# A fused two-block network on one core: four steps moved in the order of the work, and the output gates computed on 516 columns instead of 528

## The chip, the cores and the metric

The kernel runs on one core of one Trainium2 chip. The metric is the device time of one execution in microseconds (us), lower is better. A time is told as the median of several runs; the trace is one more execution, taken by the hardware profiler.

## The reference, cut to what matters

The input is a sequence of 512 positions of width 1024. A first block (gated linear attention, a gated convolution, windowed attention with sinks, then a feed-forward network with a causal convolution) gives 512 positions. The second block puts 16 meta tokens in front of them (528 positions) and computes two mixers side by side:

```
h = concat(meta_tokens, h)                       # 528 positions
q, f, i, g, z, xbc, dt = split(rmsnorm(h) @ w_in)
# HGRN2: 8 heads of 128, chunks, a state carried on
o = hgrn2(q, f, i);   y1 = rmsnorm_per_head(o) * norm_w * silu(g)
# Mamba-2: 16 heads of 64 in 2 groups
y = mamba2(silu(conv4(xbc)), softplus(dt));  y = y + d_skip * x
y = y * silu(z);      y2 = rmsnorm_per_group(y) * norm_w
h = h + concat(y1, y2) @ w_out
h = h + ffn(rmsnorm(h))                          # causal convolution, 3 taps
out = rmsnorm(h[16:])                            # the 512 positions
```

The gates g and z act position by position. Behind them only the last 4 of the 16 meta positions are read by anything that reaches the output, by way of the causal convolution of the last feed-forward network; the projections q, f, i and x, B, C feed states and need all 528.

## The kernel before

All is kept transposed, channels on the 128 partitions and positions along the free axis. The work is a list of groups (GROUPS, from plan()). One group is one output tile of 128 channels: for each 128x128 block of weights three matmuls in fp32r, w_hi·x_hi, w_lo·x_hi and w_hi·x_lo, added up in PSUM. Over 512 columns a product is one matmul; over 528 or 516 columns (from position USED = 12 on) it is two halves of 264 or 258 columns, so a group with 8 blocks issues 48 matmuls. columns(g) says which positions a group covers. The second block's groups use two PSUM slots in turn (slot_of): a group can only start when the group two before it has been evacuated.

Weights come in slabs of 8 blocks (128x1024). SyncE loads a slab into w_raw; ScalarE (ACT) copies it to w_hi in fp32r (split_until, in the profile w_hi at L911); VectorE (DVE) subtracts and stores w_lo (low_until, L1269); TensorE (PE) waits for w_lo. ACT does this at a group's own step (split_weights) and once more behind it (slab_behind), one slab further than DVE asks for at that step.

The order of everything is one hand-made list, STEPS, built by schedule(): a step "group" for each group, and behind it the stages put there. Every engine walks through the same list and issues its own part of each step, in order; semaphores tie the engines together. So a stage that stands earlier in the list stands ahead on all the engines that have a part in it.

Stages that matter here:

- hf, hq, hi, hg (heads 0 to 7): the four projections of an HGRN2 head. DVE evacuates each; ACT takes a tanh of hf, hq and hg. hf_fin, prep_ln, prep_sum and prep_exp make the decays; prep (behind hg) makes the keys and queries; head_a to head_d and head_v are the attention of the head before, on PE with copies on ACT and masks on DVE. head_b on PE waits for ACT's copies of head_a.
- second_start: part 4 is five memsets of VectorE (the largest 128x2560) that give zeros to tiles which prep and head_a of the second block fill; parts 0 to 3 scale h_res, two tiles each.
- SSM_ORDER and SSM_PIECES: the groups mz (gate), mx, mb, mc of Mamba-2, the output projections oh (of y1, 8 groups) and om (of y2, two halves of 4 blocks each), and the pieces behind each. "a t" (ssm_a): PE spreads the decays of tile t, ACT takes their exponentials, DVE multiplies; "b t" and "c t": states and outputs; "taps"/"silu": convolution; behind "c t" stand ssm_gate (DVE: two operations, the first waits for ACT's tanh of mz t), and ssm_sq (ACT squares, GpSimd adds up). ssm_sum(g) is the norm of a group: PE sums, ACT takes Ln and Exp (the root; exp_ln loads the table for it first). ssm_a(5) on PE waits for the root of group 0, since PSUM banks are shared.
- om: DVE waits for the root, multiplies the product with it (L1272), adds to h_res (L1269), and frees the slot.

Of the kernel before, what the change touches and what calls it, by code (L numbers as in the profile page):

```python
# [18 lines left out]
P = 128  # L19
D = 1024  # L20
KD = D // P
SEQ = 512
# [186 lines left out]
def schedule():  # L209
# [124 lines left out]
def program(nc, weights, xT, metaT, params, consts, cmask, w_alpha, outT):  # L334
    with ExitStack() as ctx:
# [253 lines left out]
        def _(pool):  # L589
            def ssm_sq(t):  # L590
# [5 lines left out]
                total = m_sq[:, t // 4, :]  # L596
                nc.gpsimd.tensor_tensor(total, total, m_z[t % 2], ALU.add).then_inc(ssm_sem["added"], 1)
# [7 lines left out]
        def _(pe):  # L605
# [145 lines left out]
            def head_d(n):  # L751
# [3 lines left out]
                if not gla:  # L755
                    last = mm(ps[:, 7, 416:432], ones[:, :], h_osq[:, 0:META])
# [125 lines left out]
            def ssm_sum(g):  # L882
# [4 lines left out]
                mm(ps[:, 6, 384:400], ones[:, :], m_sq[:, g, 0:META]).then_inc(S["sum"], 1)  # L887
# [15 lines left out]
        def _(act):  # L903
# [38 lines left out]
            def group(g):  # L942
                split_weights(g)
                kind, i, _ = GROUPS[g]
                if kind in ("gr", "hg"):
# [5 lines left out]
                    gate = (g_gate if kind == "gr" else h_gate)[:, i % 2, :]  # L951
                    evacuated(act, g)
                    f(c_a if kind == "gr" else h_thg, gate, ACT.Tanh, scale=0.5).then_inc(act_part, 1)
# [39 lines left out]
                elif kind == "mz":  # L993

                    if i >= 2:
                        act.wait_ge(ssm_sem["gated"], i - 1)
                    evacuated(act, g)
                    f(full[:, i % 2, :], m_z[i % 2], ACT.Tanh, scale=0.5).then_inc(act_part, 1)
# [10 lines left out]
            def group_and_slab(g):  # L1009
                group(g)  # L1010
                if GROUPS[g][0] != "hf":
# [138 lines left out]
            def head_d(n):  # L1150
# [4 lines left out]
                else:  # L1155
                    f(h_or[:, META:T2], ps[:, 6, :], ACT.Ln, scale=1.0 / P, bias=pc("eps"))
                    link(f(h_or[:, 0:META], ps[:, 7, 416:432], ACT.Ln, scale=1.0 / P, bias=pc("eps")))
                    last = f(h_or, h_or, ACT.Exp, scale=-0.5)
# [65 lines left out]
            def ssm_sq(t):  # L1224
                act.wait_ge(S["gated"], t + 1)
                out = m_z[t % 2] if t % 4 else m_sq[:, t // 4, :]
                f(out, m_y[:, t, :], ACT.Square).then_inc(S["sq"], 1)
# [3 lines left out]
            def ssm_v2(t):  # L1231
# [3 lines left out]
                f(v_hi[:, t, :], m_y[:, t, :], ACT.Identity, scale=pc("m2norm", t)).then_inc(S["v2hi"], 1)  # L1235

            def ssm_sum(g):
# [4 lines left out]
                link(f(r[:, 0:META], ps[:, 6, 384:400], ACT.Ln, scale=1.0 / SEQ, bias=pc("eps")))  # L1242
                f(r, r, ACT.Exp, scale=-0.5).then_inc(S["r"], 1)

            stages = {"raw": raw, "raw_meta": raw_meta, "slab": lambda s: split_until(s + 1), "square": square, "norm": norm, "bounds": bounds, "group": group_and_slab, "prep": prep, "prep_ln": prep_ln, "prep_exp": prep_exp, "slab_behind": slab_behind, "gate_tanh": gate_tanh, "head_a": head_a, "head_b": head_b, "head_c": head_c,
# [11 lines left out]
        def _(dve):  # L1257
# [77 lines left out]
            def group(g):  # L1335
# [6 lines left out]
                r = r_bc[:, 0:n]  # L1342
# [17 lines left out]
                elif kind in ("gr", "hg"):  # L1360
                    mul((g_gate if kind == "gr" else h_gate)[:, i % 2, :], x, r).then_inc(free, 1)
# [45 lines left out]
                elif kind == "om":  # L1407
                    g2, m = i
                    c0, c1 = columns(g)
                    dve.wait_ge(S["r"], g2 + 1)  # L1410
                    link(mul(om_r[:, c0:c1], x, m_sq[:, g2, c0:c1]))
                    tile = h_res[:, m, c0:c1]
                    tt(tile, tile, om_r[:, c0:c1], ALU.add).then_inc(free, 1)
# [450 lines left out]
```

## Time and profile before

| | us |
|---|---|
| median of 3 runs | 1803.99 |
| lowest, highest | 1803.2, 1805.36 |
| the profiled execution's own time | 1804.95 |
| its span, first to last instruction | 1803.2 |
| PE busy | 1770.3 |
| DVE busy | 1168.4 |
| ACT busy | 709.7 |

The span holds the instructions of all engines; the profiled execution's own time is 1.75 us longer. Busy is the time in which an engine has at least one instruction under way. The mean granted clock of TensorE is 0.995 of 2.4 GHz. Records of neighbouring matmuls overlap, so the start-to-start distance is shorter than one record. The first block takes about the first half of the span; the second block's HGRN2 heads run from about 878 us, its Mamba-2 part to 1411 us, and its feed-forward network from there to the end.

### The profile page before, as it was taken

Reading aid. Unit: us, or ns where it says so; the run is one execution under the profiler, and the core shown is the slowest. Engines: PE = TensorE matmul, PEld = TensorE weight load, DVE = VectorE, ACT = ScalarE, POOL = GpSimd, SP = SyncE. Lnnn points to the kernel's source line nnn. Section 1 sums busy time; section 2 is a strip of 40 time slices with the busy share of each in tenths; the row PEclk is TensorE's granted clock in tenths of the full one; section 3 lists DMA queues with packets and bytes.
Section 4 is the critical chain, followed back from the end, with each engine's and each line's share of the span. In section 5 each row is a group of like instructions: output and inputs, shape, how many; then the busy total and the mean of one; then the engine's idle time right before and its main releaser. Section 6 shows DMA issues by size and latency. Waiting matters only on the chain.

```text
span 1803.2 us, 27256 instructions
## 1 busy us (share of the span) xinstructions
PE 1770.3 (98%) x11004; PEld 1534.0 (85%) x11004; DVE 1168.4 (65%) x1798; ACT 709.7 (39%) x1085; POOL 10.4 (1%) x10
## 2 busy tenths in 40 slices
PE   8999999999999999999999999999999999999997
PEld 5777777778878888888899989999988999999885
DVE  5666656656567777633576766688788877777333
ACT  5333433332343333333545454543454433333221
POOL 0000000000000000000000000000000000000000
PEclk9999999999999999999999999999999999999998
DMA  6222222223333333332222122222212223333331
GB/s 200 79 74 79 82 82 84 82 81 94 93 87 98 96 94 93 103 96 94 70 84 71 59 69 63 70 71 63 79 60 80 74 94 94 95 94 87 101 93 59
DMA packets 44540, 154.23 MB, mean 86 GB/s; under 512 B 6000, under 2 KB 6256, under 8 KB 44416
## 3 DMA queue, kind: packets, MB, share of 16 engines
q1 hardware_dynamic: 44416, 152.50, 27.8%
q8 instruction: 87, 1.43, 0.3%
q14 instruction: 37, 0.30, 0.1%
HBM read 150.39 MB, written 2.10 MB: 85 GB/s over the span
## 4 chain that ended last, share of the span: by engine, by line
PE 81%; DVE 9%; ACT 4%; issue 2%; DVEq 1%; ACTq 1%; DMA 0%; POOL 0%; POOLq 0%; SPq 0%
PE ps L607 80%; ACT arena L911 2%; DVE arena L1272 2%; PE ps L611 2%; DVE w_lo L1269 1%; DVE arena L1279 1%; DVEq L1774 1%; ACTq L1252 1%; ACT w_hi L911 1%; DVE r_bc L1269 1%; ACT L916 0%; DVE arena L1269 0%; DVE u_lo L1464 0%; ACT u_hi L911 0%; DVE h_res L1269 0%
## 5 line engine op out<-in xcount | busy, mean ns | idle before, releaser
L607 PE MATMUL ps<-u_hi,w_hi 128*128 128x264 f32 (+3 forms) x2376 | 649.3, 326 | 12.1 <-DVE u_lo L1464 8.8
L607 PE MATMUL ps<-u_hi,w_lo 128*128 128x264 f32 (+3 forms) x2376 | 641.5, 323 | 0.0
L607 PE MATMUL ps<-u_lo,w_hi 128*128 128x264 f32 (+3 forms) x2376 | 639.9, 323 | 0.0
L607 PEld LDWEIGHTS ps<-u_hi,w_hi 128*128 128x128 f32 (+1 forms) x2376 | 395.9, 189 | 58.2 <-issue 14.7
L1269 DVE TENSOR_TENSOR w_lo<-w_raw,w_hi 128x1024 fp32r<-128x1024 f32 x280 | 342.5, 1223 | 153.6 <-ACT w_hi L911 142.2
L607 PEld LDWEIGHTS ps<-u_hi,w_lo 128*128 128x128 f32 (+1 forms) x2376 | 395.3, 188 | 36.9 <-issue 1.8
L607 PEld LDWEIGHTS ps<-u_lo,w_hi 128*128 128x128 f32 (+1 forms) x2376 | 395.1, 188 | 36.4 <-issue 0.8
L911 ACT ACTIVATE w_hi<-w_raw 128x1024 fp32r<-128x1024 f32 x280 | 294.7, 1053 | 327.4 <-PE ps L607 319.0
L1279 DVE SCALAR_TENSOR_TENSOR ffn<-full,par,ffn 128x512 f32<-128x512 f32 (+2 forms) x176 | 132.3, 751 | 81.0 <-ACT ffn L911 77.8
L911 ACT ACTIVATE arena<-arena 128x528 f32<-128x528 f32 (+10 forms) x189 | 96.5, 533 | 216.0 <-DVE arena L1272 91.8
L911 ACT ACTIVATE ffn<-full,par 128x512 f32<-128x512 f32 x88 | 67.8, 770 | 277.9 <-DVE full L1272 277.9
L607 PE MATMUL ps<-a_hi,w_lo 128*128 128x512 f32 x352 | 139.2, 396 | 0.0
L607 PE MATMUL ps<-a_lo,w_hi 128*128 128x512 f32 x352 | 139.2, 395 | 0.0
L607 PE MATMUL ps<-a_hi,w_hi 128*128 128x512 f32 x352 | 139.2, 395 | 0.0
L607 PE MATMUL ps<-arena 128*64 128x128 f32 (+13 forms) x1212 | 116.4, 274 | 4.4 <-DVE arena L1272 2.5
L607 PEld LDWEIGHTS ps<-arena 128*64 128x64 f32 (+6 forms) x1212 | 88.3, 150 | 30.0 <-issue 16.9
L1272 DVE TENSOR_TENSOR full<-ps,r_bc 128x512 f32<-128x512 f32 (+1 forms) x88 | 60.7, 689 | 42.2 <-PE ps L607 40.8
L1272 DVE TENSOR_TENSOR arena<-arena 128x512 f32<-128x512 f32 (+7 forms) x212 | 78.0, 411 | 15.2 <-ACT arena L911 13.1
L1272 DVE TENSOR_TENSOR arena<-ps,r_bc 128x528 f32<-128x528 f32 (+2 forms) x68 | 47.6, 699 | 60.7 <-PE ps L607 57.4
L607 PEld LDWEIGHTS ps<-a_lo,w_hi 128*128 128x128 f32 x352 | 66.2, 188 | 16.0
L607 PEld LDWEIGHTS ps<-a_hi,w_hi 128*128 128x128 f32 x352 | 66.2, 188 | 15.9
L607 PEld LDWEIGHTS ps<-a_hi,w_lo 128*128 128x128 f32 x352 | 66.2, 188 | 15.9
(140 smaller groups left out, 1488.2 us busy)
## 6 DMA issues: line engine op xcount, KB each, us to landing
w_raw<-weights SPq DMA_DIRECT2D x280, 512.0 KB, 3.6
h_res<-xT SPq DMA_DIRECT2D x8, 256.0 KB, 4.9
outT<-h_res SPq DMA_DIRECT2D x8, 256.0 KB, 2.1
cst<-consts SPq DMA_DIRECT2D x1, 730.0 KB, 8.6
seg<-consts SPq DMA_DIRECT2D x1, 256.0 KB, 8.7
par<-params SPq DMA_DIRECT2D x1, 240.0 KB, 5.7
msk<-cmask SPq DMA_DIRECT2D x1, 128.0 KB, 9.0
h_res<-metaT SPq DMA_DIRECT2D x1, 64.0 KB, 8.5
```

The costliest lines, as they stand in the source:

```text
L607: return nc.tensor.matmul(out, lhsT, rhs, start=start, stop=stop)
L611: return nc.tensor.transpose(out, x, ident[0:k, 0:k])
L911: return nc.scalar.activation(out, in_, func, **k)
L1252: nc.scalar.drain()
L1269: return V.tensor_tensor(out, a, b, op)
L1272: return V.tensor_tensor(out, a, b, ALU.mult)
L1279: return V.scalar_tensor_tensor(out=out, in0=a, scalar=s, in1=b, op0=ALU.mult, op1=ALU.add)
L1774: V.drain()
```

## The change

1. The memsets (second_start 4) stand behind the group hq 0 instead of hf 0.
2. Behind the group oh 2 ACT's next slab (slab_behind) comes behind its part of "a 1" instead of ahead of it.
3. Behind mz 4: ssm_sum(0), with its table load, Ln and Exp on ACT, comes first, then the tanh of mz 4 (z_tanh) and the slab; before, tanh and slab came with the group and ssm_sum(0) behind them.
4. Behind om (0, 4): the pieces are "a 7; sq 6; out 4". The evacuation of om (0, 4) on DVE (om_add) comes behind DVE's part of ssm_a(7); the square of tile 6, which stood behind mz 6, comes behind ACT's part of ssm_a(7), and with it GpSimd's add.
5. The groups hg and mz (16 groups) cover 516 columns, and the operations on h_gate, m_z, the tanh results, m_sq, h_or, and the gated outputs go over the same 516; the small matmuls for sums over meta positions have 4 columns instead of 16.

```diff
-    ("om", (0, 3)): "a 6", ..., ("mz", 6): "silu mx 7; c 6", ("om", (0, 4)): "a 7",
+    ("om", (0, 3)): "a 6", ..., ("mz", 6): "silu mx 7; c 6", ("om", (0, 4)): "a 7; sq 6; out 4",
...
-    return (USED, T2) if kind in ("oh", "om", "up2") else (0, T2)
+    return (USED, T2) if kind in ("oh", "om", "up2", "hg", "mz") else (0, T2)
...
-    put("hf", 0, ("second_start", 4))
+    put("hq", 0, ("second_start", 4))
...
-                pieces += [("ssm_sum", 0)] if n == 4 else []
+                pieces += [("ssm_sum", 0), ("z_tanh", 4), ("slab_behind", GROUP_OF[where])] if n == 4 else []
                 pieces.append(("ssm_gate", n))
                 pieces += [("ssm_v2", n)] if n == M2_T - 1 else []
-                pieces.append(("ssm_sq", n))
+                pieces += [("ssm_sq", n)] if n != 6 else []
+            if where == ("oh", 2) and stage == "a":
+                pieces.append(("slab_behind", GROUP_OF[where]))
...
-                elif kind == "mz":
...
+                elif kind == "mz" and i != 4:
+                    z_tanh(i)
+
+            def z_tanh(i):
+                if i >= 2:
+                    act.wait_ge(ssm_sem["gated"], i - 1)
+                evacuated(act, GROUP_OF[("mz", i)])
+                f(full[:, i % 2, USED:], m_z[i % 2][:, USED:], ACT.Tanh, scale=0.5).then_inc(act_part, 1)
...
             def group_and_slab(g):
                 group(g)
-                if GROUPS[g][0] != "hf":
+                if GROUPS[g][0] != "hf" and GROUPS[g][:2] not in (("mz", 4), ("oh", 2)):
                     slab_behind(g)
...
-                elif kind == "om":
...
+                elif kind == "om" and i != (0, 4):
+                    om_add(i)
...
+            def om_add(i):
+                g2, m = i
+                g = GROUP_OF[("om", i)]
+                c0, c1 = columns(g)
+                dve.wait_ge(S["r"], g2 + 1)
+                link(mul(om_r[:, c0:c1], acc(g), m_sq[:, g2, c0:c1]))
+                tile = h_res[:, m, c0:c1]
+                tt(tile, tile, om_r[:, c0:c1], ALU.add).then_inc(acc_free[slot_of(g)], 1)
```

## Rows read from the trace of the kernel before

**Rows 1.** Page, first part: busy us (share) xinstructions of each engine
```profile
PE 1770.3 (98%) x11004; PEld 1534.0 (85%) x11004; DVE 1168.4 (65%) x1798; ACT 709.7 (39%) x1085; POOL 10.4 (1%) x10
```

**Rows 2.** Windows: stretch; its us; PE, PEld, DVE, ACT, POOL busy; PEclk, DMA share, GB/s
```profile
928.00:1216.00 288.00, 288.00 (x2438) 268.01 (x2437) 198.31 (x374) 134.47 (x240) 0.00 (x0) 1.00 0.22 69
...
1295.28:1416.93 121.65, 114.39 (x959) 107.63 (x957) 107.76 (x195) 64.97 (x131) 4.82 (x3) 0.99 0.23 66
1417.00:1790.00 373.00, 373.00 (x2602) 348.62 (x2602) 218.68 (x276) 118.86 (x139) 0.00 (x0) 1.00 0.29 87
```

**Rows 3.** Waits of DVE from 1295 to 1417 us: us in total, times, longest
```profile
DVE arena L1269 <- ACT arena L911: 3.2, 2, 2.2
```

**Rows 4.** Timeline of PE where it waits: start us, us, what, count [idle before <-releaser]
```profile
899.14 0.51 PE L607 MATMUL ps<-u_hi,w_hi 128*128 128x264 f32 x2 [1.45 <-DVE arena L1272]
...
927.01 0.79 PE L607 MATMUL ps<-arena 16*128 16x128 f32 x3 [0.84 <-ACT arena L911]
...
1217.78 0.79 PE L607 MATMUL ps<-arena 16*128 16x128 f32 x3 [1.47 <-DVE arena L1272]
...
1317.59 0.50 PE L607 MATMUL ps<-ac_st,pick 32*128 32x512 f32 x4 [1.51 <-ACT arena L911]
```

**Rows 5.** Windows over hg 4 (264-column halves), oh 6 and up2 (1, 0) (258)
```profile
1024.35:1030.30 5.95, 5.95 (x51) 5.95 (x50) 5.03 (x9) 0.60 (x1) 0.00 (x0) 1.00 0.00 0
1280.54:1286.40 5.86, 5.86 (x52) 5.86 (x49) 5.13 (x8) 2.24 (x3) 0.87 (x1) 1.00 0.32 92
1424.59:1430.36 5.77, 5.77 (x51) 5.77 (x50) 4.69 (x8) 2.15 (x3) 0.00 (x0) 1.00 0.28 94
```

**Rows 6.** Timeline of DVE behind hf 0: largest memset, evacuation of hq 0, a slab
```profile
894.36 2.19 DVE L1531 MEMSET arena<- 128x2560 f32 x1 [0.66 <-issue]
...
898.38 0.70 DVE L1272 TENSOR_TENSOR arena<-ps,r_bc 128x528 f32<-128x528 f32 x1
...
900.75 1.23 DVE L1269 TENSOR_TENSOR w_lo<-w_raw,w_hi 128x1024 fp32r<-128x1024 f32 x1 [0.16 <-ACT w_hi L911]
```

**Rows 7.** Timeline of ACT ahead of head_b of head 0
```profile
922.61 1.28 ACT L911 ACT_TABLE_LOAD   x1 [2.19 <-DVE arena L1272]
...
925.58 1.38 ACT L911 ACTIVATE arena<-ps 128x512 f32<-128x512 f32 x4
```

**Rows 8.** Windows: TensorE at half clock, twice
```profile
1219.62:1223.03 3.41, 3.41 (x17) 3.41 (x17) 3.14 (x8) 0.00 (x0) 0.00 (x0) 0.50 0.26 46
1318.61:1322.02 3.41, 3.22 (x15) 2.99 (x14) 2.52 (x4) 3.12 (x10) 0.00 (x0) 0.50 0.51 149
```

**Rows 9.** Timeline of ACT and DVE: slab and ssm_a(1) behind oh 2; DVE evacuates oh 3
```profile
1211.50 1.06 ACT L911 ACTIVATE w_hi<-w_raw 128x1024 fp32r<-128x1024 f32 x1
...
1214.37 0.21 DVE L1269 TENSOR_TENSOR arena<-ps,arena 16x1 f32<-16x1 f32 x2 [0.94 <-ACT arena L911]
...
1234.59 0.70 DVE L1269 TENSOR_TENSOR h_res<-ps,h_res 128x516 f32<-128x516 f32 x1 [1.41 <-PE ps L607]
```

**Rows 10.** Timeline of ACT round mz 4: convolution's tanh, table loads, root with a square
```profile
1310.97 0.65 ACT L911 ACTIVATE arena<-arena 128x528 f32<-128x528 f32 x1 [6.96 <-DVE arena L1279]
...
1314.63 1.28 ACT L916 ACT_TABLE_LOAD   x1
...
1316.80 1.37 ACT L911 ACTIVATE arena<-arena 128x528 f32<-128x528 f32 x2
...
1327.71 1.28 ACT L911 ACT_TABLE_LOAD   x1
```

**Rows 11.** Timeline of DVE there: gate 4; ssm_a(5)
```profile
1314.76 0.71 DVE L1286 SCALAR_TENSOR_TENSOR arena<-full,arena 128x528 f32<-128x528 f32 x1
...
1322.42 0.21 DVE L1269 TENSOR_TENSOR arena<-ps,arena 16x1 f32<-16x1 f32 x2 [0.95 <-ACT arena L911]
```

**Rows 12.** Timeline of DVE round om (0, 4): its add, ssm_a(7)
```profile
1365.07 1.12 DVE L1269 TENSOR_TENSOR h_res<-h_res,arena 128x516 f32<-128x516 f32 x1
...
1366.38 0.21 DVE L1269 TENSOR_TENSOR arena<-ps,arena 16x1 f32<-16x1 f32 x2 [0.19 <-issue]
```

More of the change, by code:

```diff
@@ L755, in head_d @@
                 if not gla:
-                    last = mm(ps[:, 7, 416:432], ones[:, :], h_osq[:, 0:META])
+                    last = mm(ps[:, 7, 416:420], ones[:, :], h_osq[:, USED:META])
                 last.then_inc(st_d, 1)
@@ L886, in ssm_sum @@
                 mm(ps[:, 5, :], ones[:, :], m_sq[:, g, META:T2])
-                mm(ps[:, 6, 384:400], ones[:, :], m_sq[:, g, 0:META]).then_inc(S["sum"], 1)
+                mm(ps[:, 6, 384:388], ones[:, :], m_sq[:, g, USED:META]).then_inc(S["sum"], 1)
             def last_norm(which):
@@ L1226, in ssm_sq @@
                 out = m_z[t % 2] if t % 4 else m_sq[:, t // 4, :]
-                f(out, m_y[:, t, :], ACT.Square).then_inc(S["sq"], 1)
+                f(out[:, USED:], m_y[:, t, USED:], ACT.Square).then_inc(S["sq"], 1)
                 if t == M2_T - 1:
@@ L1241, in ssm_sum @@
                 f(r[:, META:T2], ps[:, 5, :], ACT.Ln, scale=1.0 / SEQ, bias=pc("eps"))
-                link(f(r[:, 0:META], ps[:, 6, 384:400], ACT.Ln, scale=1.0 / SEQ, bias=pc("eps")))
-                f(r, r, ACT.Exp, scale=-0.5).then_inc(S["r"], 1)
-            stages = {"raw": raw, "raw_meta": raw_meta, "slab": lambda s: split_until(s + 1), "square": square, "norm": norm, "bounds": bounds, "group": group_and_slab, "prep": prep, "prep_ln": prep_ln, "prep_exp": prep_exp, "slab_behind": slab_behind, "gate_tanh": gate_tanh, "head_a": head_a, "head_b": head_b, "head_c": head_c,
+                link(f(r[:, USED:META], ps[:, 6, 384:388], ACT.Ln, scale=1.0 / SEQ, bias=pc("eps")))
+                f(r[:, USED:], r[:, USED:], ACT.Exp, scale=-0.5).then_inc(S["r"], 1)
+            stages = {"raw": raw, "raw_meta": raw_meta, "slab": lambda s: split_until(s + 1), "square": square, "norm": norm, "bounds": bounds, "group": group_and_slab, "prep": prep, "prep_ln": prep_ln, "prep_exp": prep_exp, "slab_behind": slab_behind, "z_tanh": z_tanh, "gate_tanh": gate_tanh, "head_a": head_a, "head_b": head_b, "head_c": head_c,
                       "head_d": head_d, "swa_v": swa_v, "swa_a": swa_a, "swa_b": swa_b, "ssm_dt": ssm_dt,
@@ L1359, in group @@
                     mul(vf1 if kind == "gv" else vf2, x, r).then_inc(free, 1)
-                elif kind in ("gr", "hg"):
-                    mul((g_gate if kind == "gr" else h_gate)[:, i % 2, :], x, r).then_inc(free, 1)
+                elif kind == "gr":
+                    mul(g_gate[:, i % 2, :], x, r).then_inc(free, 1)
+                elif kind == "hg":
+                    mul(h_gate[:, i % 2, USED:], x, r).then_inc(free, 1)
                 elif kind == "hf":
@@ L1608, in prep @@
                 dve.wait_ge(act_part, PART_NO[GROUP_OF[("hg", i)]])
-                twice_silu(h_gate[:, i % 2, :], h_thg, h_gate[:, i % 2, :]).then_inc(gate2_ok, 1)
+                gate = h_gate[:, i % 2, USED:]
+                twice_silu(gate, h_thg[:, USED:], gate).then_inc(gate2_ok, 1)
             def prep_sum(n):
@@ L1650, in head_v @@
                 i = n if gla else n - GLA_H
-                o, r, gate = (g_o, g_osq, g_gate) if gla else (h_o, h_or, h_gate)
-                hi, lo = (y_hi, y_lo) if gla else (v_hi, v_lo)
+                o, r, gate = (g_o, g_osq, g_gate[:, i % 2, :]) if gla else (
+                    h_o[:, USED:], h_or[:, USED:], h_gate[:, i % 2, USED:])
+                hi, lo = (y_hi[:, i, :], y_lo[:, i, :]) if gla else (v_hi[:, i, USED:], v_lo[:, i, USED:])
                 link(V.scalar_tensor_tensor(out=o, in0=o, scalar=pc("gla_norm" if gla else "hg_norm", i), in1=r,
                                             op0=ALU.mult, op1=ALU.mult))
-                link(half_mul(o, o, gate[:, i % 2, :]))
-                parts(hi[:, i, :], lo[:, i, :], o)
+                link(half_mul(o, o, gate))
+                parts(hi, lo, o)
             def swa_a(n):
```

37 lines of the change are left out of this document (14 added, 23 removed), and 2 rows, old and new, of the table SSM_PIECES.

## The prediction, written before the changed kernel ran

> **What bounds the kernel now.** I read the page's busy times first, then windows over stages, then the waits, and last the timelines of the three engines where TensorE stands still. TensorE is busy for 98% of the span [rows 1], so a microsecond counts only where it lengthens TensorE's own chain. The windows show two kinds of stretch. From 928 to 1216 us and from 1417 to 1790 us TensorE has work in all of the time [rows 2]: there time is the number of matmuls times their distance. From 1295 to 1417 us TensorE is busy 114.4 of 121.7 us, VectorE 107.8 [rows 2], and in the list of VectorE's waits there TensorE does not occur at all; its largest wait is for ScalarE, 3.2 us in two pieces [rows 3]. So that stretch is as long as the chain of VectorE and ScalarE, and TensorE's stalls in it are only the shadow of that chain. Four stalls of TensorE touch the edits: ahead of hg 0 (1.45 us, for VectorE's evacuation of hq 0), of head_b of head 0 (0.84, for ScalarE's copies), of ssm_b(1) (1.47, for VectorE) and of ssm_a(5) (1.51, for the root) [rows 4]; a fifth, of 1.1 us ahead of ssm_b(7), lies in VectorE's stretch. I use the idle times as the rows give them.
>
> **Output gates on 516 columns.** A group of 48 matmuls on 264 columns took 5.95 us, on 258 columns 5.86 and 5.77 us [rows 5]; by columns alone it is 48 x 6 / 2.4 GHz = 0.12 us. I take 0.11 and keep 0.09 and 0.18 as ends. Of the 16 groups, hg 1 to 7 and mz 0 to 3, eleven, lie where TensorE sets the time: 11 x 0.11 = 1.2 us gained (1.0 to 2.0). hg 0 lies between two waits, mz 4 to 7 in VectorE's stretch, where their matmuls are worth nothing. There the shorter VectorE operations count: 12 elements less of 528 at 0.70 us [rows 6] are some 0.015 us, and from 1295 us on there are about 20 such operations on the chain (evacuations, gates, v_lo), with some of ScalarE and GpSimd: 0.3 us gained.
>
> **Zeros one group on.** Before, VectorE wrote the zeros (2.19 us for the largest, after 0.66 us of idle time that goes with it, and some 0.6 for the rest) between prep_sum and the evacuation of hq 0 at 898.38 [rows 6]. Without them that evacuation comes 2.8 us or more earlier, ahead of the end of hi 0, and the stall of 1.45 us goes. But the zeros are only put behind it; nothing is taken from VectorE. The slab at 900.75 comes earlier at most by the 0.16 us that VectorE waited there [rows 6]. From there on VectorE's chain is as it was: evacuation of hg 0, prep, evacuation of hf 1, its decays, evacuation of hq 1. ScalarE waits for that last one (2.19 us idle), loads its table for 1.28 us, takes the tanh, makes a slab, and only then does the four copies at 925.58 [rows 7] for which head_b waits. So head_b starts 0.15 us earlier (0 to 0.3), while TensorE gets there 1.45 + 0.1 us earlier: its stall grows from 0.84 to about 2.25 us. Gained: 0.15 us.
>
> The stall has a second price. TensorE's granted clock was 0.50, 1.2 GHz, for 3.41 us in a stretch soon after the stall of 1.47 us, and once more soon after the one of 1.51 us [rows 8, 4]; it stayed at 2.4 GHz after the one of 1.45 us. So two of three stalls of about 1.5 us were followed by a fall; one of 2.25 us should be followed by it more often. A fall: 17 matmuls in 3.41 us instead of 3.41 / 0.124 = 27 [rows 8, 5], so at least 17 x 0.124 = 2.1 us of work done, 1.3 us lost; half of 3.41 is 1.7; I take 1.5. Here it falls into the stretch where TensorE sets the time, so it is paid in full. I give it 8 in 10: this edit then costs 1.5 - 0.15 = 1.35 us.
>
> **Slab behind a tile's exponentials.** ScalarE's slab at 1211.50 takes 1.06 us; VectorE waited 0.94 us for the exponentials behind it [rows 9]. With the slab behind, they come some 1.1 us earlier and VectorE starts when its own work before is done: 0.9 us (0.87 to 0.94) earlier. All behind it on VectorE, ending in the tile for which ssm_b(1) waits, moves with it; the stall falls from 1.47 to 0.6 us. The slab itself is wanted by VectorE only at the end of ssm_a(1), some 4.5 us after its start, by when ScalarE has made it. A stall of 0.6 us leaves the clock alone: the 0.84 one did [rows 4]. So the fall of [rows 8] goes too, 1.5 us. What is late next: VectorE, busy for a further 12 us, is ahead by only 0.9 us while TensorE is ahead by 2.4; at the next point where they meet, the evacuation of oh 3, VectorE had waited 1.4 us for TensorE [rows 9], so it just keeps up. Gained: 2.4 us (0.9 if the clock falls all the same).
>
> **Root ahead of tanh and slab.** ScalarE's tanh of the convolution ends at 1310.97 + 0.65 = 1311.62. Before, the tanh of mz 4 and the slab followed, then the table load at 1314.63 and the root, until about 1317.45 (the first of the two operations at 1316.80) [rows 10]: 2.8 us. Now the root starts at 1311.7 and is there at 1314.5; TensorE's ssm_a(5) has nothing to wait for. But Ln's table does not serve tanh: after the root ScalarE loaded the other table at 1327.71, when nobody waited for it [rows 10]. That load now stands between root and tanh: 1314.5 + 1.28 + 0.65 = 1316.45. VectorE's gate 4, which started at 1314.76 [rows 11], needs this tanh: 1.7 us later, on the chain that sets the time. Behind it come the slab's low part and the evacuation of om (0, 0), which frees the slot for mx 6. So TensorE's stall is not removed but moved behind ssm_a(5) and grows to about 3.7 us. VectorE gets some back at ssm_a(5), where it waited 0.95 us for ScalarE [rows 11]; less 0.2 for the start of the stage. Cost: 1.7 - 0.75 = 0.95 us (0.5 to 1.7). The clock will fall after 3.7 us; TensorE has about so much slack until ssm_a(6) that one fall costs 0 to 0.5 us there; I count it with the next edit.
>
> The Trainium skill, "ScalarE: Activation LUTs", section "What ACT_TABLE_LOAD costs", says that a switch of set costs a drain of about 1.38 us beside the load of 1.28. By that the tanh would come 1.4 us later still and the sum below would be 1.4 us higher. The rows speak against it: the load takes 1.28 us [rows 10], and ScalarE's next operation starts where it ends.
>
> **Square and evacuation behind ssm_a(7).** ssm_a(7) starts up to 1.9 us earlier on VectorE than 1366.38 [rows 12], since the evacuation of om (0, 4) stands behind it and ScalarE no longer squares first. But what comes after, the rest of mz 7 and b 7, is as late as before: the same operations in another order. GpSimd's add lay beside the add of the evacuation, which took 1.12 us instead of 0.70 [rows 12]; it now lies beside ssm_a(7)'s last multiplications, and I expect the same there. TensorE's stall of 1.1 us goes, and it waits instead for the slot of om (0, 4) ahead of om (0, 5). Taken at 0 us (0.4 gained to 0.5 lost).
>
> The Trainium skill, "SBUF — State Buffer", section "Who interferes with whom", says that a VectorE operation with two SBUF inputs and a GpSimd one that reads SBUF exclude each other for the whole instruction. By that a multiplication could lose a whole GpSimd add, over 1 us. The 0.42 us of [rows 12] is less, for the add had been running.
>
> **Sum.** On the profiled execution: -1.2 - 0.3 (columns) - 0.15 + 1.5 (zeros) - 2.4 (slab) + 0.95 (root) + 0 = -1.6 us. Its own time was 1804.95, 0.96 above the median of 1803.99; the runs shown spread over 2.2 us, which is about what one or two falls of the clock make, so a median run may have had less of the fall that I count as gained. I put -1.6 on the median, give back 0.2 for that, and predict 1802.6 us, its own range 1801.2 to 1804.0.
>
> **Rivals.**
> - The clock does not fall ahead of head_b's successors: 1.5 us better, 1801.1. For it: the stall of 1.45 us left the clock alone. Against: 2.25 us is far more. Chance 0.15.
> - The stalls go for good. This needs VectorE's chain to be shorter than I read it, with slack where I see none. Then 1.45 (zeros), 2.4 (slab), 1.5 to 3 (root with its fall), 1.1 (om (0, 4)) and 1.2 to 2.0 (columns) are gained, 7.7 to 10: 1795 to 1796. For it: each of these waits ends last at TensorE. Against: [rows 3] and the busy VectorE of [rows 2]. All of it or a good half: 0.12.
> - Slower. The place is mx 6, waiting 3.7 us for om (0, 0)'s evacuation; the mechanism is half clock for two such spells in a row. TensorE then comes to ssm_a(6) some 1.5 us later than VectorE wants, and again to ssm_a(7): up to 2 us more, 1804.6. It decides the sign from 1.4 us on. For it: the stall is more than twice those that brought one fall. Against: none of the two falls seen was followed by a second. With the end of 1.7 us for the root or the fall behind ssm_b(1) still there it would be 1805 to 1806. Chance 0.12.
> - The slab's move does not free the clock: 1.5 us worse, 1804.1. Chance 0.05.
> - Table switch with a drain of its own, as the first page has it: 1804.0. Chance 0.03.
>
> The forecast itself has 0.53.
>
> **How the numbers follow.** 0.2% or 3.6 us is about what a measurement of this kernel can tell. Faster by more, below 1800.4, takes the second rival or the first one with the good ends of columns and slab: 0.22. Slower by more, above 1807.6, needs several prices at their far ends: 0.07. Between: 0.71. The range of 8 in 10 goes from 1799.4, halfway into the second rival, to 1804.9, over the slower one's own price.
>
> **What would show it.** Right: hg 0 follows hi 0 at once, head_b of head 0 waits about 2.2 us, and the granted clock is half in one stretch behind it; ssm_b(1) waits about 0.6 us with no half clock behind; ssm_a(5) does not wait, mx 6 waits over 3 us; a table load stands directly behind the root, and gate 4 waits for the tanh; a group hg takes 5.84 us. Wrong: head_b's wait stays below 1.2 us (VectorE had slack at the zeros), or gate 4 does not wait, or VectorE shows waits for TensorE between 1295 and 1417 us.

## The result, and the profile after

The changed kernel takes 1806.28 us (median of 21 runs, 1803.36 to 1808.24) against 1804.05 us of the kernel before in the same session (21 runs, 1802.88 to 1806.1): ratio 1.0013, 95% interval 1.0007 to 1.0019. It is slower by about 2.2 us where I had forecast 1802.6, and lies outside the range of 8 in 10. Its profiled execution took 1805.75 us (span 1804.0).

The busy times of the page after answer to [rows 1]: 0.7 us less work on TensorE and on VectorE, and a longer span.

```profile
PE 1769.6 (98%) x11004; PEld 1533.9 (85%) x11004; DVE 1167.7 (65%) x1798; ACT 709.3 (39%) x1085; POOL 10.3 (1%) x10
```

TensorE's waits after, the answer to [rows 4] (start us, us, what, idle before, releaser):

```profile
926.95 1.35 PE L609 MATMUL ps<-arena 16*128 16x128 f32 x8 [2.47 <-ACT arena L913]
...
1317.25 0.51 PE L609 MATMUL ps<-u_hi,w_hi 128*128 128x264 f32 x2 [3.51 <-DVE h_res L1273]
...
1370.26 0.80 PE L609 MATMUL ps<-v_hi,w_hi 128*128 128x258 f32 x2 [2.68 <-DVE h_res L1273]
```

The stalls of 1.45, 1.47 and 1.51 us are gone. In their place stand 2.47 us ahead of head_b of head 0, 3.51 us ahead of mx 6 and, new, 2.68 us ahead of om (0, 5), which waits for its slot. (The wait ahead of ssm_b(1) is 0.68 us.) Windows after, over hg 4 and over the two stretches at half clock ahead of the end, answer to [rows 5] and [rows 8]:

```profile
1023.80:1029.64 5.84, 5.84 (x52) 5.84 (x51) 5.14 (x9) 0.60 (x1) 0.00 (x0) 1.00 0.00 0
1318.42:1321.83 3.41, 3.41 (x18) 3.41 (x17) 2.84 (x8) 1.88 (x11) 0.00 (x0) 0.50 0.02 7
1369.62:1376.44 6.82, 6.18 (x28) 6.18 (x29) 4.74 (x11) 1.19 (x2) 0.00 (x0) 0.50 0.25 78
```

Behind the 2.47 us ahead of head_b this execution kept 2.4 GHz. VectorE, which never waited for TensorE in this part before, now does so once, 1.44 us ahead of its evacuation of om (0, 5):

```profile
1375.82 0.69 DVE L1276 TENSOR_TENSOR arena<-ps,arena 128x516 f32<-128x516 f32 x1 [1.44 <-PE ps L609]
```

Where the time went shows when one follows the start of a group in both traces. hg 1: 928.49 after, 928.55 before. oh 3: 1225.28 against 1228.53, 3.2 us ahead. mz 4: 1296.94 against 1300.40, 3.5 ahead. mx 6: 1317.25 against 1319.03, 1.8 ahead. mz 7: 1360.29 against 1362.61, 2.3 ahead. om (0, 5): 1370.26 against 1370.89. om (1, 0): 1384.07 against 1381.96, 2.1 behind, and up2 (0, 0) 1411.61 against 1411.29, 0.3 behind. So in this execution edits 1, 2 and 5 brought 3.5 us, edit 3 took 1.2 to 1.7 of it, and between mz 7 and om (1, 0), where I had expected nothing, the rest was lost.

### The profile page after: what moved, and what is told of

Same layout as the page of the kernel before. It is cut to its first block, busy times and chain, and to the rows that moved or that the text cites. A ratio compares the mean times of both kernels' runs of the same rounds, so it can differ in the third digit from the quotient of the medians.

```text
span 1804.0 us, 27259 instructions
## 1 busy us (share of the span) xinstructions
PE 1769.6 (98%) x11004; PEld 1533.9 (85%) x11004; DVE 1167.7 (65%) x1798; ACT 709.3 (39%) x1085; POOL 10.3 (1%) x10
## 3 DMA queue, kind: packets, MB, share of 16 engines
q8 instruction: 87, 1.43, 0.3%
## 4 chain that ended last, share of the span: by engine, by line
PE 84%; DVE 8%; ACT 4%; issue 1%; DVEq 1%; ACTq 1%; DMA 0%; SPq 0%
PE ps L609 83%; DVE arena L1276 2%; ACT arena L913 2%; PE ps L613 2%; DVE w_lo L1273 1%; DVEq L1787 1%; ACTq L1256 1%; DVE arena L1283 1%; ACT w_hi L913 1%; DVE r_bc L1273 1%; ACT L918 0%; DVE arena L1273 0%; DVE u_lo L1474 0%; ACT u_hi L913 0%; DVE h_res L1286 0%
## 5 line engine op out<-in xcount | busy, mean ns | idle before, releaser
L609 PE MATMUL ps<-u_hi,w_hi 128*128 128x258 f32 (+3 forms) x2376 | 647.8, 326 | 14.1 <-DVE u_lo L1474 8.9
L609 PE MATMUL ps<-u_hi,w_lo 128*128 128x258 f32 (+3 forms) x2376 | 640.3, 323 | 0.0
L609 PE MATMUL ps<-u_lo,w_hi 128*128 128x258 f32 (+3 forms) x2376 | 639.0, 322 | 0.0
L913 ACT ACTIVATE arena<-arena 128x528 f32<-128x528 f32 (+11 forms) x189 | 96.3, 532 | 212.6 <-DVE arena L1276 90.9
L1276 DVE TENSOR_TENSOR arena<-ps,r_bc 128x516 f32<-128x516 f32 (+3 forms) x68 | 47.3, 696 | 60.5 <-PE ps L609 57.2
```

What stands on the lines that cost most here:

```text
L609: return nc.tensor.matmul(out, lhsT, rhs, start=start, stop=stop)
L913: return nc.scalar.activation(out, in_, func, **k)
L1276: return V.tensor_tensor(out, a, b, ALU.mult)
```

## The experiments

My theory after the result: each part does to the order of work about what the prediction says, but a stall of TensorE that is made longer brings a fall of the clock with a price of its own, and edit 4 costs time by itself. (A stretch at half clock, 1.2 GHz, is called a spell below. In the texts of undo_om and undo_root theory A holds edit 4 for the dearest part, theory B edit 3.) The rivals: one edit alone did it (the zeros, or the root); or the parts are harmless and only the slab's move failed.

### Undo one edit in the changed kernel

Each diff is cut to its main line. What belongs to the edit is put back with it: in undo_root the tanh and the slab of mz 4, in undo_slab the slab of oh 2, in undo_om the square and the evacuation.

```diff
--- undo_zeros
-    put("hq", 0, ("second_start", 4))
+    put("hf", 0, ("second_start", 4))
--- undo_slab
-            if where == ("oh", 2) and stage == "a":
-                pieces.append(("slab_behind", GROUP_OF[where]))
--- undo_root
-                pieces += [("ssm_sum", 0), ("z_tanh", 4), ("slab_behind", GROUP_OF[where])] if n == 4 else []
+                pieces += [("ssm_sum", 0)] if n == 4 else []
--- undo_om
-    ... ("om", (0, 4)): "a 7; sq 6; out 4",
+    ... ("om", (0, 4)): "a 7",
...
```

> The changed kernel with edit 1 undone: the memsets behind hf 0 again. Theory A: the wait ahead of head_b of head 0 goes back from about 2.5 to 0.9 us; VectorE's chain is the same, so what is saved is the fall of the clock that follows the longer wait in most executions though not in the profiled one: 0.5 to 1.5 us less than the changed kernel, 1804.8 to 1805.8. Rival: the fall of the clock does not come there, as in the profiled execution: the same time as the changed kernel or 0.1 us more, 1806.3.

> The changed kernel with edit 2 undone: ScalarE's slab ahead of its part of ssm_a(1). Theory A: the wait ahead of ssm_b(1) is 1.5 us again, 0.9 us more than in the changed kernel, and the clock falls behind it in some executions (up to 1.5 us more): 1807.2 to 1808.7. Rival (the gain there is given back later, since VectorE is the bound from 1295 us on): less than 0.5 us more than the changed kernel.

> The changed kernel with edit 3 undone: tanh of mz 4 and the slab ahead of the root. Both theories have VectorE's gate 4 waiting no more and mx 6 starting about 1.7 us earlier. Theory A: only 0.5 to 1.2 us less than the changed kernel (1805.1 to 1805.8), for VectorE had got back part of it at ssm_a(5). Theory B: 2 us or more less, at or below 1804.3.

> The changed kernel with edit 4 undone: behind om (0, 4) the evacuation and the square stand where they stood before. Theory A (edit 4 is the dearest part: GpSimd's add blocks VectorE's last multiplication for 1.1 us, then TensorE waits 2.7 us for the slot, its clock falls and VectorE waits for it): 2.0 to 2.8 us less than the changed kernel, about 1803.8, and no wait above 0.5 us ahead of om (0, 5). Theory B (edit 3, root ahead of tanh, is the dearest part and edit 4 is about nothing, as predicted): within 0.5 us of the changed kernel, 1805.8 to 1806.8.

Measured (11 runs each; the kernel before was 1804.01 beside them): undo_zeros 1803.92 (1803.11 to 1806.39), undo_slab 1808.04 (1805.35 to 1810.02), undo_root 1804.3 (1802.61 to 1804.73), undo_om 1805.36 (1803.42 to 1806.61). Read against 1806.28: the zeros cost 2.4 us, the root 2.0, edit 4 cost 0.9, and the slab gains 1.8. The slab did not fail, and by the medians no single edit did it. Of what I expected, undo_slab came; undo_root came out at theory B's number; undo_om saved more than theory B and less than half of what theory A said; undo_zeros saved 0.9 us more than its range. The intervals of these ratios are 3.2 us wide, so 2.4 and 2.0 are likely prices and 0.9 alone is none. The later kernels have intervals as wide; what tells the prices apart there is the traces. In undo_slab TensorE's stall ahead of ssm_b(1) is back at 1.43 us; with the slab moved (cols_slab, below) it is 0.68:

```profile
1218.34 1.35 PE L607 MATMUL ps<-arena 16*128 16x128 f32 x8 [1.43 <-DVE arena L1274]
```

```profile
1216.05 1.35 PE L609 MATMUL ps<-arena 16*128 16x128 f32 x8 [0.68 <-DVE arena L1276]
```

### Fill the stall instead of removing it

If the clock has a price of its own, work that nobody needs, put into the stall, must give it back without moving any chain.

```diff
--- fill_head_b (the changed kernel)
+                pe.wait_ge(attn_ok, n + 1)
+                if n == GLA_H:
+                    for _ in range(11):
+                        mm(ps[:, 4, 0:3 * BLK], u_hi[:, 0, 0:P], u_hi[:, 0, 0:3 * BLK])
                 pe.wait_ge(tok_ok, n + 1)
-                pe.wait_ge(attn_ok, n + 1)
--- fill_om (the changed kernel)
                 last.then_inc(S["B"], 1)
+                if t == M2_T - 1:
+                    pe.wait_ge(S["decay"], t + 1)
+                    for _ in range(12):
+                        mm(ps[:, 5, :], u_hi[:, 0, 0:P], u_hi[:, 0, META:T2])
```

The first block's four heads are counted too: n == GLA_H, head 4 of all, is head 0 of the second block.

> The changed kernel with 11 matmuls on 384 columns, whose result nobody reads, put on TensorE ahead of head_b of head 0, where it waits about 2.5 us for ScalarE's copies; the wait's end is the same. Theory A (the clock falls behind that wait in most executions, and this is what edit 1 costs): no fall there, 1.0 to 1.5 us less than the changed kernel, about 1805.1, close to the kernel with edit 1 undone (1803.9). Rival (edit 1 costs by something else, VectorE's order of work): the same time as the changed kernel.

> The changed kernel with 12 matmuls on 512 columns, whose result nobody reads, put on TensorE behind ssm_b(7), where it would wait for the slot of om (0, 4); nothing else is changed and the wait's end is the same. Theory A (the wait itself costs little, the fall of the clock behind it makes TensorE late for VectorE): no half clock near 1370 us, om (0, 5) takes 2.9 us instead of 5.1, VectorE does not wait for TensorE behind it: 1.0 to 2.0 us less than the changed kernel, about 1804.8. Rival (the wait for the slot alone is what costs): the same time as the changed kernel, 1806.3, or more.

Measured: fill_head_b 1804.53 (1803.89 to 1805.71), 1.75 us below the changed kernel; fill_om 1804.9 (1803.5 to 1807.08), 1.4 below. Neither profile has a half clock at its filled place. The chain got nothing: in fill_om om (0, 5) starts 10.02 us after mz 7 (9.97 unfilled), in fill_head_b head_b 29.36 us after hg 0 (29.35 unfilled). By these medians both stalls cost by the clock, 1.4 to 1.8 us each. The filled place of fill_om, ahead of om (0, 5) and behind its start:

```profile
1369.00:1372.40 3.40, 3.40 (x18) 2.58 (x17) 3.18 (x5) 0.60 (x1) 1.27 (x1) 1.00 0.00 0
1372.40:1375.80 3.40, 3.40 (x30) 3.40 (x29) 2.85 (x9) 1.33 (x2) 0.00 (x0) 1.00 0.43 136
```

### The two halves of edit 4

```diff
--- om_evac_only (the square stays behind mz 6)
-    ("om", (0, 4)): "a 7; sq 6; out 4"
+    ("om", (0, 4)): "a 7; out 4"
--- om_sq_only (the evacuation stays with its group)
+    ("om", (0, 4)): "a 7; sq 6"
```

> The changed kernel with only the half of edit 4 that moves the evacuation of om (0, 4); the square and with it GpSimd's add stay behind mz 6. Theory A: GpSimd's add no longer lies beside ssm_a(7)'s multiplications, which take 1.45 us again instead of 2.5, but ScalarE's exponentials come 0.8 us later; TensorE still waits over 2 us for the slot and its clock falls in most executions: 1805.2 to 1806.3. Rival (the blocked multiplication is the whole price): as with edit 4 undone, 1805.4 or less, and no half clock behind the wait.

> The changed kernel with only the half of edit 4 that moves the square of tile 6 and with it GpSimd's add behind ssm_a(7); the evacuation of om (0, 4) stays ahead. Theory A: the multiplications take 2.5 us again (blocked by the add), but TensorE does not wait for the slot: 0.3 to 0.8 us more than with edit 4 undone (1805.4), 1805.7 to 1806.2. Rival (the slot's wait is the whole price): 1805.4 or less.

Measured: 1805.69 (1805.15 to 1807.62) and 1805.18 (1802.91 to 1806.57), 0.6 and 1.1 us below the changed kernel; against undo_om's 1805.36 that is no difference, so the times do not say which half costs what. The rows show what each half does: VectorE's last multiplications of ssm_a(7) with the evacuation alone (first fence) and with the square alone (second), and GpSimd's add beside the latter.

```profile
1368.85 1.45 DVE L1276 TENSOR_TENSOR arena<-arena 128x512 f32<-128x512 f32 x4 [0.52 <-ACT arena L913]
```

```profile
1369.15 2.57 DVE L1276 TENSOR_TENSOR arena<-arena 128x512 f32<-128x512 f32 x4 [0.52 <-ACT arena L913]
1369.91 1.78 POOL L599 TENSOR_TENSOR arena<-arena 128x516 f32<-128x516 f32 x1 [28.13 <-ACT arena L913]
```

The square's half makes the multiplications 1.1 us longer, whenever GpSimd's add starts among them. The evacuation's half makes om (0, 5) wait for its slot (2.14 us idle, with a spell of 3.41 us behind it), and without the other half VectorE's ssm_a(7) waits 1.20 us for ScalarE, which squares first. From the start of mz 7 to that of up2 (0, 0) the square alone takes 49.3 us and the evacuation alone 49.9, where undo_om takes 48.3. So om_sq_only, whose median came out at the number of its rival (the slot's wait is the whole price), does not bear that rival out: its multiplications cost 1.0 us of chain without any wait for the slot.

### Build up from the two edits that were not in doubt

Five kernels are made of the undo diffs above: cols_only is the changed kernel with all four undone, cols_slab with three (zeros, root, om), cols_slab_root with zeros and om, cols_slab_zeros with root and om, cols_slab_om with zeros and root. The sixth, cols_slab_zeros_fill, adds to cols_slab_zeros, at the place of fill_head_b (the wait for tok_ok follows behind it, as there):

```diff
+                if n == GLA_H:
+                    for _ in range(15):
+                        mm(ps[:, 4, 0:3 * BLK], u_hi[:, 0, 0:P], u_hi[:, 0, 0:3 * BLK])
```

> Edit 5 alone, the output gates on 516 columns. 11 groups at 0.11 us, and 0.3 in VectorE's stretch: 1.5 us less than before, 1802.6, with before's spread by falls of the clock. Rival (columns are worth nothing, the whole gain of 3.2 us of edits 2 and 5 is the slab's): 1804.

> Edits 2 and 5 alone (slab behind ssm_a(1)'s exponentials, 516 columns); edits 1, 3 and 4 undone. Theory A (these two gain, the other three lose): 1.2 us for 11 groups on 516 columns, 0.9 us for the wait plus up to 1.5 for the fall of the clock behind it that no longer comes, 0.3 in VectorE's stretch: 2.4 to 3.9 us less than before, 1800.1 to 1801.6. Rival (gains ahead of 1295 us are lost again in VectorE's stretch): 1803 or more.

> Edits 2 and 5 with edit 3 added (root ahead of tanh and slab); 1 and 4 undone. It gives the price of edit 3 by itself against the kernel with 2 and 5 alone (1800.9). Theory A: VectorE's gate 4 waits 2 us for the tanh, half of it is given back at ssm_a(5): 1.0 us more, plus up to 0.5 where the clock falls for two spells behind the wait of 3.8 us: 1801.9 to 1802.5. Rival (edit 3 costs nothing without edit 4): 1800.9 to 1801.3.

> The kernel before with the 516 columns, the slab behind a tile's exponentials and the zeros one group on (edits 5, 2 and 1), root and evacuation as before. The version without the zeros' move measured 1800.9 us and showed no half clock before the end. Theory (a longer stall ahead of head_b of head 0 costs its clock fall, and nothing else): hg 0 follows hi 0 at once, head_b of head 0 resumes at about 926.5 us as in every version with this edit, so 0.1 us comes from the chain and a half-clock spell behind 927 us adds 1.4 (3.41 us long) to 2.5 us (6.83 us long): 1802.2 to 1803.3 us, about 1.0009 of it or more. Rival A (the zeros' move costs only in company of the falls that root and evacuation bring): 1800.8 us, no spell. Rival B (it costs more than the clock, by a chain made longer): over 1803.3 us and head_b of head 0 resuming over 0.5 us later than in the version without it.

> The same with 15 extra matmuls of 384 columns ahead of head_b of head 4, in time in which TensorE waits for the exponentials, their result used by nothing. Theory (the price is the clock's): no half clock at 927 us, head_b of head 0 resuming within 0.3 us of the kernel without them, and the time back at 1800.8 to 1801.5 us, 1.4 to 2.5 below its companion. Rival B (the chain is longer by itself): the same time as its companion, with or without the spell.

> The kernel before with the 516 columns, the slab behind the exponentials and the evacuation one place on (edits 5, 2 and 4), root and zeros as before. The version without edit 4 measured 1800.9 us. Theory: ssm_a(7) comes early, but om (0,5) waits for its slot because VectorE's last multiplications take 1 us more beside GpSimd's add; half clock at 1370 us or not, up2 (0,0) starts 0.2 to 1.5 us later than without the edit: 1801.5 to 1802.5 us. Rival (edit 4 costs only because root's move made mx 6 stall and fall before it): 1800.9 us or less, up2 (0,0) no later than without the edit.

| kernel | edits | median (range), us | against cols_slab |
|---|---|---|---|
| cols_only | 5 | 1803.18 (1801.63 to 1804.26) | +2.28 |
| cols_slab | 5, 2 | 1800.9 (1800.72 to 1801.96) | 0 |
| cols_slab_root | 5, 2, 3 | 1802.55 (1802.07 to 1803.75) | +1.65 |
| cols_slab_zeros | 5, 2, 1 | 1802.41 (1800.52 to 1803.62) | +1.51 |
| cols_slab_zeros_fill | 5, 2, 1, fill | 1801.41 (1800.51 to 1801.69) | +0.51 |
| cols_slab_om | 5, 2, 4 | 1802.79 (1801.91 to 1805.15) | +1.89 |

cols_slab and cols_slab_zeros came out in their ranges, cols_slab_root at the edge of its own, cols_slab_om 0.3 us above, cols_only 0.6 above its number. cols_slab's profile has no half clock ahead of 1791 us; its ratio to the kernel before is 0.9982 (0.9973 to 0.9991). 1800.9 + 1.65 + 1.51 + 1.89 = 1805.95, where 1806.28 was measured, so the three prices nearly add up. But the kernels come from three sessions, in which the kernel before took 1804.16 us (cols_slab), 1804.65 (cols_only, cols_slab_root) and 1804.27 (the other three). Taken against their own sessions the prices are 1.2 (root), 1.4 (zeros) and 1.8 (edit 4), the slab gains 1.8, and 1.1 us of the way from cols_slab to the changed kernel stay without a price. So the medians are good to about half a microsecond. Against cols_slab's trace the price of each edit can be read row by row.

**Zeros.** cols_slab_zeros: TensorE's wait ahead of head_b of head 0, and the window behind it.

```profile
926.99 1.35 PE L609 MATMUL ps<-arena 16*128 16x128 f32 x8 [2.50 <-ACT arena L913]
```

```profile
926.99:940.00 13.01, 13.01 (x106) 12.74 (x107) 7.97 (x23) 4.48 (x8) 0.00 (x0) 1.00 0.29 82
```

cols_slab has that matmul at 926.97: the chain gained and lost nothing. This profiled execution kept its clock behind the stall, and took 1801.0 us, 0.2 more than the profiled one of cols_slab (1800.84); the median is 1.5 above. The filled kernel gives back 1.0 of it, which was less than the 1.4 I had put down; 0.5 stays unexplained. What a spell costs at this place shows in the traces where it came, as in undo_om:

```profile
928.05:931.46 3.41, 3.41 (x19) 3.41 (x17) 2.56 (x5) 0.60 (x1) 0.00 (x0) 0.50 0.31 120
```

From head_b's start to that of ssm_b(1) it is 288.9 to 289.1 us in the nine kernels with the slab moved whose trace has no spell there, 290.5 to 290.7 in the four with 3.41 us of it, and 291.9 in undo_root with 6.83. The price is 1.4 to 1.6 us and 2.8.

**Root.** VectorE's gate 4, ssm_a(5) and ssm_a(6), first in cols_slab, then in cols_slab_root:

```profile
1311.26 0.70 DVE L1290 SCALAR_TENSOR_TENSOR arena<-full,arena 128x516 f32<-128x516 f32 x1
...
1318.91 0.21 DVE L1273 TENSOR_TENSOR arena<-ps,arena 16x1 f32<-16x1 f32 x2 [0.99 <-ACT arena L913]
...
1342.02 0.21 DVE L1273 TENSOR_TENSOR arena<-ps,arena 16x1 f32<-16x1 f32 x2 [0.19 <-issue]
```

```profile
1313.25 0.70 DVE L1290 SCALAR_TENSOR_TENSOR arena<-full,arena 128x516 f32<-128x516 f32 x1 [1.97 <-ACT full L913]
...
1320.32 0.21 DVE L1273 TENSOR_TENSOR arena<-ps,arena 16x1 f32<-16x1 f32 x2 [0.54 <-issue]
...
1343.81 0.21 DVE L1273 TENSOR_TENSOR arena<-ps,arena 16x1 f32<-16x1 f32 x2 [0.55 <-ACT arena L913]
```

mz 4 starts 0.11 us later in the second kernel, so gate 4 is 1.88 us late, ssm_a(5) 1.30, ssm_a(6) 1.68. Between the last two VectorE is 1.3 us late through and through and then waits 0.55 for ScalarE's exponentials, which wait for TensorE: it comes late, since mx 6 ran at half clock (window of 6.83 us below; it begins in the stall) and took 8.08 us instead of 5.83.

```profile
1315.56:1322.39 6.83, 5.00 (x22) 5.00 (x23) 5.96 (x13) 5.09 (x19) 0.00 (x0) 0.50 0.29 78
```

**Edit 4.** VectorE from the last multiplications of ssm_a(7) on, and up2 (0, 0) on TensorE, first cols_slab, then cols_slab_om:

```profile
1366.58 1.45 DVE L1276 TENSOR_TENSOR arena<-arena 128x512 f32<-128x512 f32 x4 [0.52 <-ACT arena L913]
1368.13 1.23 DVE L1273 TENSOR_TENSOR w_lo<-w_raw,w_hi 128x1024 fp32r<-128x1024 f32 x1
...
1372.38 0.70 DVE L1276 TENSOR_TENSOR arena<-ps,arena 128x516 f32<-128x516 f32 x1 [0.16 <-issue]
...
1373.89 0.75 DVE L1777 SCALAR_TENSOR_TENSOR v_lo<-arena,par,v_hi 128x516 fp32r<-128x516 f32 x1
...
1407.52 0.51 PE L609 MATMUL ps<-u_hi,w_hi 128*128 128x258 f32 x2 [1.14 <-DVE h_res L1273]
```

```profile
1364.96 2.53 DVE L1276 TENSOR_TENSOR arena<-arena 128x512 f32<-128x512 f32 x4 [0.52 <-ACT arena L913]
...
1369.06 0.80 PE L609 MATMUL ps<-v_hi,w_hi 128*128 128x258 f32 x2 [2.69 <-DVE h_res L1273]
1369.10 1.22 DVE L1273 TENSOR_TENSOR w_lo<-w_raw,w_hi 128x1024 fp32r<-128x1024 f32 x1
...
1373.66 0.70 DVE L1276 TENSOR_TENSOR arena<-ps,arena 128x516 f32<-128x516 f32 x1 [0.47 <-PE ps L609]
...
1375.68 0.75 DVE L1777 SCALAR_TENSOR_TENSOR v_lo<-arena,par,v_hi 128x516 fp32r<-128x516 f32 x1 [0.59 <-ACT v_hi L913]
...
1409.37 0.50 PE L609 MATMUL ps<-u_hi,w_hi 128*128 128x258 f32 x2 [1.15 <-DVE h_res L1273]
```

The second kernel starts mz 7 0.09 us later. The slab is then 0.97 us late (the multiplications' 1.08), the evacuation of om (0, 5) 1.28, since it now waits for TensorE, which stood 2.69 us for the slot and then ran at half clock for 3.41 us, and v_lo 1.79, since ScalarE, behind its slab and TensorE's delay, has v_hi late. up2 (0, 0) is late by 1.85 us and the median by 1.89. The stall on TensorE, with its spell, had become the bound of VectorE's chain.

undo_root has edit 4 too, and the same stall, but its trace has no spell behind it:

```profile
1371.74 0.51 PE L609 MATMUL ps<-v_hi,w_hi 128*128 128x258 f32 x2 [2.69 <-DVE h_res L1273]
```

This splits the price. The times from the start of mz 7 to that of up2 (0, 0), in all the traces but the two with one half of the edit (49.3 and 49.9, above), are:

| edit 4 | half clock behind the stall of om (0, 5), us | mz 7 to up2 (0, 0), us |
|---|---|---|
| none (8 kernels) | no such stall | 48.2 to 48.7 |
| both halves (undo_root; fill_om, filled) | none | 49.4, 49.5 |
| both halves (cols_slab_om, fill_head_b) | 3.41 | 50.3, 50.3 |
| both halves (changed kernel, undo_zeros, undo_slab) | 6.83 | 51.2 to 51.3 |

So 0.9 us (49.4 against 48.5 in cols_slab) comes without any fall, about what the multiplications lose; a spell of 3.41 us adds 0.9, one of 6.83 us 1.8.

### Zeros off VectorE's chain

The row that explains the zeros also says what to do: they should go to an engine with nothing to do. pool_zeros is cols_slab with the five memsets on GpSimd, at the step of the first block's last group, as soon as the root of the norm ahead of the second block is there.

```diff
+                if kind == "group" and GROUPS[i][:2] == ("down", KD - 1):
+                    pool.wait_ge(rstd_ok, NORMS.index("norm1") + 1)
+                    for tile in (KC, h_attn, h_am, h_step, h_head):
+                        nc.gpsimd.memset(tile, 0.0).then_inc(zeros_ok, 1)
...
-                    V.memset(KC, 0.0)            # and the other four, on VectorE
+                    dve.wait_ge(zeros_ok, 5)     # this step now stands behind hi 0
```

> As the kernel with edits 2 and 5 alone, and the zeros written by GpSimd, which is idle there, from the end of the norm ahead of hf 0 on; VectorE only waits for them behind hi 0. Theory A (edit 1 did not help because the zeros stayed on VectorE's chain; taken off it, both waits go): neither hg 0 nor head_b of head 0 waits over 0.3 us, 2.4 us less than the kernel with edits 2 and 5 alone, about 1798.5. Rival (the chain to head_b is ScalarE's, or GpSimd's writes slow VectorE): at most 1 us less.

```profile
886.55 2.85 POOL L607 MEMSET arena<- 128x2560 f32 x5 [886.12 <-ACT r_bc L917]
...
925.17 1.35 PE L613 MATMUL ps<-arena 16*128 16x128 f32 x8 [0.76 <-ACT arena L917]
```

1798.64 us (1798.35 to 1798.83, 5 runs), ratio 0.9968 (0.9956 to 0.9981): 2.3 us below cols_slab, 5.5 below the kernel before, the best of all, and the time that I had expected. hg 0 follows hi 0 at once and the wait ahead of head_b does not grow: ScalarE's copies themselves come 1.8 us earlier (925.17 against 926.97), for now VectorE's work is really less. I had expected head_b to wait at most 0.3 us; it waits 0.76, for ScalarE. The stretch from mz 4 to up2 (0, 0) is 0.7 us shorter than in cols_slab as well, and no run says why. No half clock ahead of the end.

## Why the prediction was wrong

**The reading of the stage chains held.** All signs in its last part came but one: hg 0 follows at once, head_b waits 2.47 us (2.2 predicted), ssm_b(1) waits 0.68 in cols_slab (0.6), mx 6 waits 3.51 (over 3), the table load stands behind the root, gate 4 waits for tanh, hg 4 takes 5.84 us. The one that did not: the profiled execution has no half clock behind head_b of head 0, as the first rival had it (chance 0.15). That the median run pays it I take from the 1.75 us that fill_head_b gives back.

**Columns, -1.5, and slab, -2.4: right.** cols_only is 1.47 us below the kernel before of its session. In its trace head_b to mz 4 is 1.12 us shorter (ssm_b(1) to oh 3, where the spell of the kernel before lies, left out) and mz 4 to up2 (0, 0) 0.28; 1.2 and 0.3 were predicted. The slab's stall gives 0.76 (0.9 predicted), and the spell behind it is worth the 1.5 that I took: ssm_b(1) to oh 3 takes 10.76 us before and 9.24 without it. But cols_only and undo_slab, with the same stall, show no spell there, so a median run has less of it to lose. The profiled execution of cols_slab took 1800.84 us, 4.1 less than that of the kernel before (3.9 predicted); cols_only to cols_slab is 2.28 on medians. By medians the two edits bring 3.15 (1804.05 to 1800.9). The profiled execution that I summed against had more of the falls than a median run; I gave back 0.2 for that where about 0.75 was due.

**Zeros, +1.35: right alone.** 1.51 in cols_slab_zeros (1.4 by its session). The 0.15 us of chain was 0, and a spell of 3.41 us costs 1.4 to 1.6, where I took 1.5. The chance was right too: of the eight kernels with edit 1 and an unfilled stall of about 2.5 us, six show a half clock behind it in their profile, of the seven with a stall of 0.76 to 0.87 us none. In the full kernel undoing it gives 2.4, and in undo_root the spell there was 6.83 us long, where I had allowed for 3.41.

**Root, +0.95: too small, 1.65 measured.** The step that was mis-sized is what ssm_a(5) gives back: 0.45 us (VectorE's wait there went from 0.99 to 0.54), not 0.75; and gate 4 was 1.88 late instead of 1.7. With it ssm_a(5) is 1.30 late. The fall that I had put at "0 to 0.5" and counted with the next edit, at 0, is the other 0.4. That the rows of mx 6 would show one spell of 3.41 us held in five of nine kernels with this edit; the other four, and none of the eight without it, had 6.83 us.

The Trainium skill, "ScalarE: Activation LUTs", section "What ACT_TABLE_LOAD costs", had a switch of set cost 1.38 us more. ScalarE's rows after show the load of 1.28 us between root and tanh, and nothing else that long:

```profile
1310.40 0.64 ACT L913 ACTIVATE arena<-arena 128x516 f32<-128x516 f32 x1
1311.16 1.28 ACT L913 ACT_TABLE_LOAD   x1
1312.45 0.64 ACT L913 ACTIVATE full<-arena 128x516 f32<-128x516 f32 x1
```

**Edit 4, taken at 0: this step failed.** It costs 1.89 us in cols_slab_om and by medians 0.9 in the full kernel, where the stretch from mz 7 on is 2.8 us longer in the profiled execution than in that of cols_slab (51.3 against 48.5). The prediction has the two facts that decide it, and let both go. First: "GpSimd's add ... now lies beside ssm_a(7)'s last multiplications, and I expect the same there", 0.42 us. But in [rows 12] GpSimd's add had begun 1.2 us before VectorE's add (at 1363.87, for 1.77 us), and only its rest was in the way; here it begins amid the multiplications and takes 1.08 us of them (1.45 to 2.53). It is what the Trainium skill, "SBUF — State Buffer", section "Who interferes with whom", has as an exclusive lock for a whole instruction, and my sentence beside that rule, over 1 us, was the right one; GpSimd's add took 1.74 us, and the multiplications lost 1.1 of them. Second: "it waits instead for the slot of om (0, 4)": I gave the new stall no length and no fall. It is 2.7 us long, and of the seven kernels with both halves that leave it empty or the evacuation's half alone, six show a half clock behind it. VectorE, which bounds this stretch, then waits for TensorE's om (0, 5), once, and the shadow had become the bound. That was one of my own signs for "wrong". The first fact is worth 0.9 us, the second 0.9 with a spell of 3.41 us and 1.8 with one of 6.83.

**The sum.** Forecast to result is 3.7 us: edit 4 1.9, root 0.7, zeros 0.15, too little given back for the falls of the profiled execution 0.55. Some 0.4 us remain with no step to it; it is well within the errors (the intervals of the ratios make 2 to 4.5 us), as is the root's 0.7: by its session it would be 0.2, by the rows (mz 4 to up2 (0, 0) 1.74 us longer in cols_slab_root) 0.8. (In the second rival the gains of 7.7 to 10 us lead to 1794 to 1796.3, not 1795 to 1796.)

**The rival of the slower side** had its place (mx 6) and its mechanism (spells in a row) right in four kernels of nine, but its price by itself was 0.4 in cols_slab_root, not 2. In the four kernels mx 6 to mz 7 takes 43.7 to 44.2 us, in the five with one spell of 3.41 us 43.0 to 43.1. What tipped the sum was the place where I had priced nothing, with the root's excess.

**Not settled:** why undoing the zeros in the full kernel gives 2.4 us and in the clean one 1.5, and undoing edit 4 0.9 against 1.9, when the profiled executions of the changed kernel and of undo_om differ by 2.2 from mz 4 to up2 (0, 0). The spells of half clock change their place and length from execution to execution, and one profile for each kernel does not tell their mean.

## What to carry to other kernels

Ahead of a move, write down for every stall of the matmul engine whether it goes or only wanders; one that wanders and grows can have the price of the clock on top, here 1.4 to 2.8 us at head_b and 0.9 to 1.8 at om (0, 5) for each fall, and it is paid in full where matmuls set the time. Moving work to a later place of the same full engine bought nothing (zeros, root); moving it to an engine that idles bought 2.3 us. An edit that is taken at zero because "the same operations only change their order" needs two more looks: which operations now overlap on a shared resource, and how long the wait is that it creates.

## What the runs showed of the hardware that I had not expected

- The length of a half-clock spell varies: 3.41 us or 6.83 us, behind stalls of like length and even in kernels that differ elsewhere (at mx 6 behind 3.5 us: five times 3.41, four times 6.83).
- A single spell of 3.41 us may cost nothing: in cols_slab_zeros, mx 6 ran through one and took 7.27 us instead of 5.83, and mx 7 began at 1339.52, against 1339.44 without it.
- A GpSimd add with both inputs in SBUF that begins amid a run of VectorE multiplications of 128x512, also from SBUF, costs them 1.08 to 1.12 us; beside one that had been running an add lost 0.39 to 0.42.
- How often the clock fell hung on more than the length of the stall. Behind 1.4 to 1.5 us it fell in none of six traces at hg 0, in one of three at ssm_b(1) and in five of eight at ssm_a(5); behind 3.5 us at mx 6 in nine of nine.
- Matmuls whose result nobody reads, in a stall, kept the granted clock at 2.4 GHz in three of three profiles and brought 1.0 to 1.75 us.
